# A two-layer decoder trunk in fp32: new order of work at the start, at the layer's jump, at the end of each feed-forward part and in the last norm

## Chip, cores, metric

The kernel runs on one core of one Trainium2 chip. The metric is the device time of one execution in microseconds (us), the median over several runs.

## What is computed

The reference is a decoder trunk of two layers over 1024 prompt positions and 8 sample positions, 1032 columns in all, with 1024 features. Cut to what matters here:

```python
for l in range(DEPTH):                      # DEPTH = 2
    h = _rmsnorm(x, w['norm_mix_g'][l])
    proj = jnp.einsum('bld,de->ble', h, w['w_in'][l])
    ...                                     # RG-LRU | retention | SSD heads on slices of proj
    x = x + jnp.einsum('blm,md->bld', mix, w['w_out'][l])
    h = _rmsnorm(x, w['norm_ffn_g'][l])
    gu = jnp.einsum('bld,df->blf', h, w['ffn_w_up'][l])
    gate, up = gu[..., :D_FF], gu[..., D_FF:]           # D_FF = 2816
    gate, ffn_buf = _causal_dwconv(gate, st_ffn_conv[l], w['ffn_conv_w'][l], w['ffn_conv_b'][l])
    x = x + jnp.einsum('blf,fd->bld', jax.nn.gelu(gate) * up, w['ffn_w_down'][l])
y = _rmsnorm(x, w['norm_final_g'])
```

The states of the convolutions and of the three recurrences are outputs too.

## The kernel before

Activations lie transposed: 128 features on the partitions, 1032 columns along a row, `x` as eight such tiles. Every large product is made in three passes of the tensor engine on numbers split into a high and a low part (`three`: w_hi by h_hi, w_hi by h_lo, w_lo by h_hi), over column groups of 344, so 9 matmul instructions of 128x344 for each pair of a weight tile and an activation tile (`three_wide`). The weights come in slots of 128x1024 (8 weight tiles): SP loads slot s into `w_raw[s % 2]`, GpSimd splits it into `w_hi` and `w_lo` (L649, L652), TensorE uses it and gives it free (`w_used0`, `w_used1`). There are 110 slots in a layer: 32 of the input projection, 12 of the output projection and 66 of the feed-forward part. So GpSimd can split a slot only when TensorE has left the one two before it.

The norm is not applied to `h`: ScalarE makes `h_hi` = x by gain (L1052) and the squares (L1048), VectorE makes `h_lo` (L1318) and adds the squares up in `rstd` (L1312, L1315). TensorE sums them over the partitions (`token_sums`, L750), VectorE and ScalarE take the root (`token_norm`), TensorE spreads the result over the partitions (`spread_rstd`, L759), and VectorE multiplies products by it when it takes them out of PSUM (`evict`, L1349).

A layer runs like this. (1) The first two input slots, tiles 24 and 25, are made together: for each feature tile k first slot 1, then slot 0 (from L913 on). Both are taken out of PSUM by VectorE with the factor `rstd` (L1631, L1633). Ahead of them stand the token sums, the `dt` products (L931) and the spread. (2) The other input slots and the output slots are dealt by a planner (`schedule`, `PLAN`) to six units of recurrent work, L0, L1 (RG-LRU), S0, S1 (SSD), R0, R1 (retention); projected tiles go to DRAM (`proj`) and are loaded again into `raw` or `pt` for convolutions and gates. SP issues all these loads in one queue, in program order, with a wait ahead of each: `load_conv` waits for `conv_done` where it uses a buffer again, and weight loads (`weights`, L373) stand behind it. (3) The feed-forward part: 11 blocks of 256 features. The loop makes, in each of its 10 turns, the four up slots of block b+1 and then the two down slots of block b (4 output tiles each). The two down slots of the last block come behind the loop. VectorE and ScalarE turn an up result into `y_hi`, `y_lo` (`up_part`, `y_part`, `ffn_block`) and VectorE adds each down result to `x` (L1834, L1843). Behind the last block `refresh` makes the next norm's squares and `h_hi`, `h_lo` tile by tile between those additions. After two layers the last norm follows, and eight tiles of output leave by `ev`, a buffer of two (L1853).

At the layer's jump the first two slots of the next layer are split by GpSimd like all others; the second one's buffer is given free at the very end of the layer (L1029 to L1030):

```python
            pe.wait_ge(sg.sem("m_ready"), layer * RUSES + RUSES)
            pe.nop().then_inc(sg.sem("w_used1"), 1)
```

and TensorE begins the layer with a wait for slot 1 and for all of PSUM (L911, L912).

## Time and profile before

| | us |
|---|---|
| median of 3 runs | 2965.53 (2960.07 to 2966.77) |
| profiled execution, its own time | 2957.84 |
| its span, first to last instruction | 2955.9 |
| TensorE busy in the span | 2836.5 (96%) |
| VectorE busy | 1645.2 (56%) |
| GpSimd busy | 1019.8 (35%) |
| ScalarE busy | 582.0 (20%) |
| mean granted TensorE clock | 0.979 of full |

The sum of the prediction is made against the profiled execution. Its time stands 7.7 us below the median of the runs. Busy times are shares of the whole span; the difference of span and busy time on TensorE, 119 us, lies in a few stretches and many short gaps.

### The profile page before, as it was taken

What the parts mean: (1) busy time and instruction counts of PE and PEld (TensorE: products, weight loads), DVE (VectorE), ACT (ScalarE), POOL (GpSimd) and SP (SyncE); (2) the same over time, 40 slices, a digit from 0 to 9 for tenths busy, and PEclk for the clock granted to TensorE, in tenths of its full rate; (3) what the DMA queues carried; (4) which work ended last, traced back from release to release, by engine and by line L of the source; (5) the groups of instructions that cost most, each with busy time, mean ns of one, the idle gap of its engine ahead of it and who ended that gap; (6) DMA issues with size and microseconds to landing.
All of it is one profiled execution on the core that took longest, in us unless ns stands there. A gap on an engine that the chain in (4) does not pass through costs nothing.

```text
span 2955.9 us, 46968 instructions
## 1 busy us (share of the span) xinstructions
PE 2836.5 (96%) x18164; PEld 2772.3 (94%) x18164; DVE 1645.2 (56%) x2122; ACT 582.0 (20%) x887; POOL 1019.8 (35%) x444
## 2 busy tenths in 40 slices
PE   7999999989999999999799999999999999999995
PEld 6999999979999999999789999988899999999995
DVE  4658886366444544444645587855664444444446
ACT  3333231113100111111213342211221111100002
POOL 2433233213343434444324333231233444434340
PEclk9999999989999999999999999999999999999997
DMA  4324334311111111111123234244011111111112
GB/s 154 114 78 144 108 123 160 121 61 38 51 44 49 44 49 50 43 50 43 54 79 105 93 137 138 96 151 138 30 46 49 50 43 50 43 50 43 50 43 77
DMA packets 75816, 227.94 MB, mean 77 GB/s; under 512 B 18672, under 2 KB 19696, under 8 KB 74624
## 3 DMA queue, kind: packets, MB, share of 16 engines
q1 hardware_dynamic: 73760, 219.77, 22.4%
q10 hardware_dynamic: 1920, 6.34, 0.7%
q8 instruction: 86, 1.41, 0.2%
q14 instruction: 50, 0.41, 0.0%
HBM read 180.63 MB, written 45.96 MB: 77 GB/s over the span
## 4 chain that ended last, share of the span: by engine, by line
PE 86%; DVE 7%; issue 4%; DMA 1%; ACT 1%; PEld 1%; POOL 0%; SPq 0%; DVEq 0%; ACTq 0%; POOLq 0%; PEldq 0%
PE ps L670 26%; PE ps L672 25%; PE ps L671 25%; PE ps L780 1%; DVE sb_pt L1362 1%; PE ps L838 1%; PE ps L803 1%; PE ps L901 1%; DVE sb_x L1352 1%; PE ps L884 0%; PE ps L815 0%; PE ps L814 0%; PE ps L902 0%; PE ps L759 0%; DMA sb_ch<-cos 0%
## 5 line engine op out<-in xcount | busy, mean ns | idle before, releaser
L670 PE MATMUL ps<-sb_h_hi,sb_w_hi 128*128 128x344 f32 x3744 | 1215.1, 325 | 32.0 <-DVE sb_h_lo L1318 15.1
L671 PE MATMUL ps<-sb_h_lo,sb_w_hi 128*128 128x344 f32 x3744 | 1201.6, 321 | 0.0
L672 PE MATMUL ps<-sb_h_hi,sb_w_lo 128*128 128x344 f32 x3744 | 1201.3, 321 | 0.0
L649 POOL TENSOR_TENSOR sb_w_hi<-sb_w_raw,sb_ones 128x1024 fp32r<-128x1024 f32 x220 | 426.9, 1941 | 1861.3 <-PEq L1011 877.9
L670 PEld LDWEIGHTS ps<-sb_h_hi,sb_w_hi 128*128 128x128 f32 x3744 | 709.6, 190 | 41.6 <-issue 16.7
L671 PEld LDWEIGHTS ps<-sb_h_lo,sb_w_hi 128*128 128x128 f32 x3744 | 709.4, 189 | 1.1
L672 PEld LDWEIGHTS ps<-sb_h_hi,sb_w_lo 128*128 128x128 f32 x3744 | 709.4, 189 | 0.0
L652 POOL TENSOR_TENSOR sb_w_lo<-sb_w_raw,sb_w_hi 128x1024 fp32r<-128x1024 f32 x220 | 592.8, 2695 | 17.3
L670 PE MATMUL ps<-sb_y_hi,sb_w_hi 128*128 128x344 f32 x1536 | 508.9, 331 | 37.3 <-DVE sb_y_lo L1824 12.3
L672 PE MATMUL ps<-sb_y_hi,sb_w_lo 128*128 128x344 f32 x1536 | 497.3, 324 | 0.0
L671 PE MATMUL ps<-sb_y_lo,sb_w_hi 128*128 128x344 f32 x1536 | 494.2, 322 | 0.0
L1834 DVE TENSOR_TENSOR sb_x<-ps,sb_x 128x1032 f32<-128x1032 f32 x160 | 197.2, 1233 | 256.1 <-PE ps L672 256.1
L670 PEld LDWEIGHTS ps<-sb_y_hi,sb_w_hi 128*128 128x128 f32 x1536 | 292.4, 190 | 46.0 <-issue 21.6
L671 PEld LDWEIGHTS ps<-sb_y_lo,sb_w_hi 128*128 128x128 f32 x1536 | 293.0, 191 | 1.1
L672 PEld LDWEIGHTS ps<-sb_y_hi,sb_w_lo 128*128 128x128 f32 x1536 | 292.8, 191 | 0.0
L1349 DVE TENSOR_TENSOR sb_ev<-ps,sb_rstd 128x344 f32<-128x344 f32 x180 | 89.6, 511 | 237.9 <-PE ps L672 219.5
L1283 ACT ACTIVATE sb_y_hi<-sb_pt 128x1032 fp32r<-128x1032 f32 x44 | 47.1, 1071 | 804.0 <-DVE sb_pt L1820 803.9
L1794 DVE TENSOR_TENSOR sb_raw<-ps,sb_rstd 128x1032 f32<-128x1032 f32 x44 | 54.3, 1234 | 254.6 <-PE ps L672 254.3
L1812 DVE TENSOR_TENSOR sb_pt<-ps,sb_rstd 128x1032 f32<-128x1032 f32 x44 | 54.2, 1233 | 232.8 <-PE ps L672 232.8
L1352 DVE TENSOR_TENSOR sb_x<-ps,sb_x 128x344 f32<-128x344 f32 x264 | 126.8, 509 | 54.9 <-PE ps L672 54.3
L1801 DVE SCALAR_TENSOR_TENSOR sb_pt<-sb_raw,sb_par,sb_pt 128x1024 f32<-128x1024 f32 x88 | 129.4, 1470 | 7.2 <-DVE sb_pt L1804 6.2
L1276 ACT ACTIVATE sb_pt<-sb_raw,sb_par 128x1032 f32<-128x1032 f32 x44 | 55.3, 1256 | 328.0 <-DVE sb_raw L1794 328.0
(243 smaller groups left out, 2222.0 us busy)
## 6 DMA issues: line engine op xcount, KB each, us to landing
sb_w_raw<-w SPq DMA_DIRECT2D x222, 512.0 KB, 3.5
proj<-sb_ev SPq DMA_DIRECT2D x64, 516.0 KB, 3.5
sb_raw<-proj SPq DMA_DIRECT2D x32, 516.0 KB, 4.5
sb_pt<-proj SPq DMA_DIRECT2D x28, 516.0 KB, 6.6
sb_ch<-cumT SPq DMA_DIRECT2D x32, 256.0 KB, 4.0
sb_x<-x SPq DMA_DIRECT2D x8, 516.0 KB, 8.7
y<-sb_ev SPq DMA_DIRECT2D x8, 516.0 KB, 2.7
sb_raw<-ssd_state SPq DMA_DIRECT2D x4, 1024.0 KB, 6.3
```

Of the source, the lines that this page charges most:

```text
L649: nc.gpsimd.tensor_tensor(w_hi[:, q, :], w_raw[:, q, :], ones[:, 0:1].to_broadcast([P, 1024]), ALU.mult).then_inc(sg.sem("w_hi_done"), 1)
L652: nc.gpsimd.tensor_tensor(w_lo[:, q, :], w_raw[:, q, :], w_hi[:, q, :].bitcast(F32), ALU.subtract).then_inc(*sg.on("w_split_done", q))
L670: mm(o, wh, ah, start=first, stop=False)
L671: mm(o, wh, al, start=False, stop=False)
L672: return mm(o, wl, ah, start=False, stop=last)
L1276: af(pt[:, j, :], raw[:, j, 2:T + 2], ACT.Identity, bias=wt[3], scale=wt[2]).then_inc(*sg.on("ffn_tap", (tag, j)))
L1349: v.tensor_tensor(ev[:, EV[i], gc(g)], o, rstd[:, gc(g)], ALU.mult).then_inc(*sg.on(f"p_free{r % NB}", r))
L1352: v.tensor_tensor(x[:, mo, gc(g)], o, x[:, mo, gc(g)], ALU.add).then_inc(*sg.on(f"p_free{r % NB}", r))
L1794: v.tensor_tensor(g3(raw[:, j, 2:T + 2]), ffn_bank(r)[:, :, 0:TG], g3(rstd[:]), ALU.mult).then_inc(*sg.on("m_free", ("ffn", r)))
L1801: stt(pt[:, j, 0:SEQ], raw[:, j, k:k + SEQ], w, pt[:, j, 0:SEQ], ALU.mult, ALU.add).then_inc(*line.step())
L1812: v.tensor_tensor(g3(pt[:, 2 + j, :]), ffn_bank(r)[:, :, 0:TG], g3(rstd[:]), ALU.mult).then_inc(*sg.on("m_free", ("ffn", r)))
L1834: v.tensor_tensor(g3(x[:, mo, :]), ffn_bank(r)[:, :, 0:TG], g3(x[:, mo, :]), ALU.add).then_inc(*sg.on("m_free", ("ffn", r)))
```

## The change

It does the following.

- Start: SP loads weight slot 0 first, ScalarE's own queue loads `x` tile 0, slot 1 comes behind `x` tile 3. ScalarE and VectorE split slots 0 and 1 of the first layer; GpSimd starts with the third slot. `h_hi` and `h_lo` of all tiles come before the squares and their sums. TensorE runs 20 products of `ones` by `ones` (128x128) ahead of its first work.
- First two slots of each layer: slot 0 with tiles 0 to 3, slot 1 with tiles 0 to 3, slot 0 with tiles 4 to 7, slot 1 with tiles 4 to 7. TensorE starts them without the last PSUM bank group and with slot 0 alone. The last sum of squares is added at the layer's top (`sums_done`). ScalarE takes tiles 24 and 25 out of PSUM without `rstd`, and VectorE multiplies them in SBUF later (`t0_scaled`, `t1_scaled`). The spread comes behind the first piece of tile 26.
- Loads: the second use of `raw` in units L0, L1 (gates) and S0, S1 (convolution tiles 2 and 3) is issued by ScalarE instead of SP. In S0, S1 `silu` of tile 1 comes ahead of the tap of tile 2.
- End of the feed-forward part: the loop has 9 turns. Then: the last block's four up slots; the first down slot of block 9; the first down slot of block 10, on `y` parts that are kept in `h_hi`, `h_lo` tiles 6 and 7; and two slots "both", each with two output tiles summed over the four feature tiles of both blocks in PSUM. The number of matmul instructions is the same; `x` gets 12 additions there instead of 16.
- Last norm: the token sum is made in two parts, seven tiles' squares and the last tile's; the spread goes to PSUM banks 0 to 2 in two steps, VectorE reads it there, and the eight output tiles have eight places (`ev` and six of `pt`), the first and the last in two parts.

The core of the difference:

```diff
+        sp.dma_start(w_raw[:, 0, :], io["w"][0]).then_inc(sg.sem("w_raw0"), 16)
         sp.dma_start(gains[:], io["gains"]).then_inc(*sg.on("gains_loaded", None, 16))
-        sp.dma_start(w_raw[:, 0, :], io["w"][0]).then_inc(sg.sem("w_raw0"), 16)
-        sp.dma_start(x[:, 0, :], io["x"][0]).then_inc(*sg.on("x_loaded0", None, 16))
-        sp.dma_start(w_raw[:, 1, :], io["w"][1]).then_inc(sg.sem("w_raw1"), 16)
         for m in range(1, KD):
             sp.dma_start(x[:, m, :], io["x"][m]).then_inc(*sg.on(f"x_loaded{m}", None, 16))
+            if m == 3:
+                sp.dma_start(w_raw[:, 1, :], io["w"][1]).then_inc(sg.sem("w_raw1"), 16)
...
-                if u < 4:
-                    for j in (2, 3):
-                        load_conv(u, j, t0 + j)
...
+        pairs = DEPTH * SLOTS // 2 - 1
+        with pool.Fori(0, pairs) as i, sg.loop("split", pairs, i):
+            for q in range(2):
+                pool.wait_ge(sg.sem(f"w_raw{q}"), i * 16 + 32)
+                pool.wait_ge(sg.sem(f"w_used{q}"), i + (1 + q))
...
+        pe.wait_ge(*sg.after("ones_ready"))
+        for _ in range(20):
+            mm(ps[:, 3, 0:128], ones[:], ones[:], start=True, stop=True)
         with pe.Fori(0, DEPTH) as layer, sg.loop("layer", DEPTH, layer):
+            def tile_k(bank0, q, k, last):
+                w = slice(k * P, (k + 1) * P)
+                return three_wide(ps[:, bank0:bank0 + 3, :], w_hi[:, q, w], w_lo[:, q, w], h_hi[:, k, :], h_lo[:, k, :],
+                                  k == 0, last)
...
+            slot_ready(0)
+            pe.wait_ge(sg.sem("m_free"), layer * RUSES + (M0 - 1))
+            for k in range(4):
+                pe.wait_ge(sg.sem("h_split"), layer * (2 * KD) + (k + 1))
+                ins = tile_k(4, 0, k, False)
+                if k == 0:
+                    ins.then_inc(sg.sem("w_used1"), 1)
             slot_ready(1)
             pe.wait_ge(sg.sem("m_free"), layer * RUSES + M0)
-            for k in range(KD):
+            for k in range(4):
+                tile_k(0, 1, k, False)
+            for k in range(4, KD):
                 pe.wait_ge(sg.sem("h_split"), layer * (2 * KD) + (k + 1))
-                w = slice(k * P, (k + 1) * P)
-                ins = three_wide(ps[:, 0:3, :], w_hi[:, 1, w], w_lo[:, 1, w], h_hi[:, k, :], h_lo[:, k, :],
-                                 k == 0, k == KD - 1)
-                if k == KD - 1:
-                    ins.then_inc(*sg.on("t1_ready"))
-                ins = three_wide(ps[:, 4:7, :], w_hi[:, 0, w], w_lo[:, 0, w], h_hi[:, k, :], h_lo[:, k, :],
-                                 k == 0, k == KD - 1)
+                ins = tile_k(4, 0, k, k == KD - 1)
             ins.then_inc(*sg.on("t0_ready"))
+            for k in range(4, KD):
+                ins = tile_k(0, 1, k, k == KD - 1)
+                if k == 4:
+                    ins.then_inc(sg.sem("w_used0"), 1)
+            ins.then_inc(*sg.on("t1_ready"))
...
+            pe.wait_ge(*sg.after("sums_done"))
+            token_sums("mix", "w_used1")
             pe.wait_ge(*sg.after("wdt_ready"))
             for k in range(KD):
                 for g, (c0, n) in enumerate(DT):
                     ins = mm(ps[32 * g:32 * g + 8, 3, 0:n], A("wdt", 8 * k, 8), x[:, k, c0:c0 + n],
                              start=k == 0, stop=k == KD - 1)
             ins.then_inc(*sg.on("dt_done"))
-            pe.wait_ge(*sg.after("dt_taken"))
-            spread_rstd("mix")
             pe.wait_ge(*sg.after("t1_free"))
             run([("in", 26, 0)])
...
+            run([("in", 26, 1)])
+            pe.wait_ge(*sg.after("rstd_ready", "mix"))
...
+                n, pieces = {"up": (KD, 1), "down": (2, 4), "down_last": (2, 4), "both": (4, 2)}[kind]
...
+            for j in range(4):
+                ffn_slot("up", j % 2, END + 4 + j, 0, SLOTS - 8 + j)
+            pe.wait_ge(sg.sem("ffn_split"), layer * FB + (FB - 1))
+            ffn_slot("down", 0, END + 8, 0, SLOTS - 4)
             pe.wait_ge(sg.sem("ffn_split"), layer * FB + FB)
+            ffn_slot("down_last", 1, END + 12, 0, SLOTS - 3)
             for j in range(2):
-                ffn_slot("down", j, 4 + 4 * j, 12 * (FB - 1), 48 + j, 6 * (FB - 1))
-            pe.wait_ge(sg.sem("m_ready"), layer * RUSES + RUSES)
-            pe.nop().then_inc(sg.sem("w_used1"), 1)
-        pe.wait_ge(sg.sem("h_split"), (2 * DEPTH + 1) * KD)
+                ffn_slot("both", j, END + 16 + 2 * j, 0, SLOTS - 2 + j)
...
+        pe.wait_ge(*sg.after("sq_used", ("next", KD - 2)))
+        token_sums("most")
+        pe.wait_ge(*sg.after("sq_tile", ("next", KD - 1)))
+        for c in range(NCH + 1):
+            s = slice(c * CHUNK, min((c + 1) * CHUNK, T))
+            ins = mm(ps[0:s.stop - s.start, 3, c:c + 1], ev[:, 1, s], ones[:, 0:1], start=True, stop=True)
+        ins.then_inc(*sg.on("tok_sum", "last"))
         pe.wait_ge(sg.sem("m_free"), DEPTH * RUSES + M0)
-        token_sums("last")
-        spread_rstd("last")
+        for _ in range(4):
+            mm(ps[:, 4, 0:128], ones[:], ones[:], start=True, stop=True)
+        pe.wait_ge(*sg.after("tok_rstd", "last"))
+        for c in range(NCH + 1):
+            n = min(CHUNK, T - c * CHUNK)
+            o = ps[:, c // 4, (c % 4) * CHUNK:(c % 4) * CHUNK + n]
+            ins = mm(o, rt[0:n, c:c + 1].to_broadcast([n, P]), ident[0:n, 0:n], start=True, stop=True)
+            if c in (3, NCH):
+                ins.then_inc(*sg.on("spread", c // 4 - c // NCH))
...
+        def load_s(u, j):
+            tile = TILE0[UNITS[u]] + j
+            act.wait_ge(*sg.after(f"ev_stored{EV[tile]}", tile))
+            act.wait_ge(*sg.after("conv_done", (u, j - 2)))
+            act.dma_start(raw[:, j - 2, 3:T + 3],
+                          io["proj"][tile]).then_inc(*sg.on(f"raw_turn{j - 2}", (u, j), 16))
...
+        act.dma_start(x[:, 0, :], io["x"][0]).then_inc(*sg.on("x_loaded0", None, 16))
+        act.wait_ge(*sg.after("ones_ready"))
+        af(rgc[:, 0, 0:1], ones[:, 0:1], ACT.Square)
+        act.wait_ge(sg.sem("w_raw0"), 16)
+        af(w_hi[:, 0, :], w_raw[:, 0, :], ACT.Identity).then_inc(*sg.on("first_hi", 0))
         act.wait_ge(*sg.after("gains_loaded"))
         for m in range(KD):
+            if m == 4:
+                act.wait_ge(sg.sem("w_raw1"), 16)
+                af(w_hi[:, 1, :], w_raw[:, 1, :], ACT.Identity).then_inc(*sg.on("first_hi", 1))
             act.wait_ge(*sg.after(f"x_loaded{m}"))
-            refresh(m, 0, "start")
+            part(m, 0, "start")
+        for m in range(KD):
+            square(m, "start")
...
+            act.wait_ge(*sg.after("t0_ready"))
+            af(g3(ev[:, 0, :]), ps[:, 4:7, 0:TG], ACT.Identity).then_inc(*sg.on("t0_free"))
+            act.wait_ge(*sg.after("t1_ready"))
+            af(g3(ev[:, 1, :]), ps[:, 0:3, 0:TG], ACT.Identity).then_inc(*sg.on("t1_free"))
...
+                load_s(u, 2)
                 silu(u, 0)
+                load_s(u, 3)
+                silu(u, 1)
                 tap_s(u, 2)
-                silu(u, 1)
...
+        def first_lo(q):
+            dve.wait_ge(sg.sem(f"w_raw{q}"), 16)
+            dve.wait_ge(*sg.after("first_hi", q))
+            if q == 0:
+                dve.wait_ge(sg.sem("w_split_done"), FREE)
+            v.tensor_tensor(w_lo[:, q, :], w_raw[:, q, :], w_hi[:, q, :].bitcast(F32),
+                            ALU.subtract).then_inc(sg.sem("w_split_done"), 1)
+        first_lo(0)
         dve.wait_ge(*sg.after("gains_loaded"))
         for m in range(KD):
+            if m == 4:
+                first_lo(1)
             dve.wait_ge(*sg.after(f"x_loaded{m}"))
-            refresh(m, 0, "start")
+            part(m, 0, "start")
+        for m in range(KD - 1):
+            add_square(m, "start")
...
+            v.tensor_tensor(rstd[:], rstd[:], ev[:, 1, :], ALU.add).then_inc(*sg.on("sums_done"))
...
+            up_part(FB - 1, "end", END + 4, 0)
+            y_product("end", END + 7, 0)
+            for mo in range(2):
+                down(mo, END + 8 + mo, 0, "end")
+            y_rest("end")
+            for mo in range(2, 4):
+                down(mo, END + 8 + mo, 0, "end")
+            dve.wait_ge(*sg.after("ffn_split", "end"))
             v.nop().then_inc(*sg.on("par_free"))
             for mo in range(KD):
-                r = 4 + mo
-                dve.wait_ge(sg.sem("m_ready"), layer * RUSES + 12 * (FB - 1) + (r + 1))
-                v.tensor_tensor(g3(x[:, mo, :]), ffn_bank(r)[:, :, 0:TG], g3(x[:, mo, :]),
-                                ALU.add).then_inc(*sg.on("m_free", ("last", r)))
-                if mo >= 1:
+                if mo < 4:
+                    dve.wait_ge(sg.sem("m_free"), layer * RUSES + (END + 9 + mo + M0))
+                if mo == KD - 1:
+                    add_square(mo - 1, "next")
+                down(mo, END + 12 + mo, 0, "last")
+                if mo == KD - 1:
+                    part(mo - 1, layer * 2 + 2, "next")
+                elif mo >= 1:
                     refresh(mo - 1, layer * 2 + 2, "next")
-            refresh(KD - 1, layer * 2 + 2, "next")
-        token_norm("last")
-        take_rstd("last")
+            part(KD - 1, layer * 2 + 2, "next")
...
+        wide = ps[:, 0:3, :].rearrange("p a n -> p (a n)")
         for m in range(KD):
-            if m >= 2:
-                dve.wait_ge(*sg.after(f"y_stored{m % 2}", m - 2))
-            stt(ev[:, m % 2, :], x[:, m, :], gains[:, 2 * DEPTH * KD + m:2 * DEPTH * KD + m + 1], rstd[:],
-                     ALU.mult, ALU.mult).then_inc(*sg.on("y_ready", m))
+            gp = gains[:, 2 * DEPTH * KD + m:2 * DEPTH * KD + m + 1]
+            for n, s in enumerate(parts(m)):
+                if m == 0:
+                    dve.wait_ge(*sg.after("spread", n))
+                stt(out_tile(m)[:, s], x[:, m, s], gp, wide[:, s], ALU.mult, ALU.mult).then_inc(*sg.on("y_ready", (m, n)))
...
+        rows = [256 * b + P * k for b in (FB - 2, FB - 1) for k in range(2)]
         seq = ups(0)
-        for b in range(FB - 1):
+        for b in range(FB - 2):
             seq += ups(b + 1) + downs(b)
-        seq += downs(FB - 1)
+        seq += ups(FB - 1) + [downs(FB - 2)[0], downs(FB - 1)[0]]
+        seq += [fin_slot(down, rows, (4, 5)), fin_slot(down, rows, (6, 7))]
```

Below, names of the kernel before and after are as the programs print them; `[waits ...]` names semaphores, and a line number is one of the kernel it comes from. 
SP at the start of unit S0 (`sb_raw<-proj` are the convolution's tiles, `sb_pt<-proj` the gates, `sb_w_raw<-w` weight slots), before:

```order
L423 DMA sb_raw<-proj 128x1032 [waits conv_done]
L423 DMA sb_raw<-proj 128x1032 [waits ev_stored1,conv_done]
L482 ISA
L400 REGISTER_ALU [waits y_split]
L430 DMA sb_pt<-proj 128x1032 [waits ev_stored0]
L430 DMA sb_pt<-proj 128x1032 [waits ev_stored1]
L559 ISA
L497 DMA sb_ch<-cumT 128x512 [waits cumT_stored]
L497 DMA sb_ch<-cumT 128x512 x2
L395 REGISTER_ALU
L397 DMA proj<-sb_ev 128x1032 [waits p_free2]
L371 REGISTER_ALU
```

and after (`L442` loads the gates now, `L388` the weights):

```order
L479 ISA
L415 REGISTER_ALU [waits y_split]
L442 DMA sb_pt<-proj 128x1032 [waits ev_stored0]
L442 DMA sb_pt<-proj 128x1032 [waits ev_stored1]
L553 ISA
L494 DMA sb_ch<-cumT 128x512 [waits cumT_stored]
L494 DMA sb_ch<-cumT 128x512 x2
L410 REGISTER_ALU
L412 DMA proj<-sb_ev 128x1032 [waits p_free2]
L386 REGISTER_ALU
L388 ISA [waits w_split_done]
L388 DMA sb_w_raw<-w 128x1024
```

The two loads with `conv_done` ahead of them are gone from SP, and the next weight load (the DMA that follows the rows shown before, the last row after) waits for no convolution any more.

VectorE from the last turn of the feed-forward loop into what follows it, before (`L1834` and `L1843` add a down result to `x`):

```order
L1833 REGISTER_ALU
L1834 TENSOR_TENSOR sb_x<-ps,sb_x 128x1032 [waits m_ready]
L1820 TENSOR_TENSOR sb_pt<-sb_pt 128x1032 [waits ffn_gelu,m_free]
L1820 TENSOR_TENSOR sb_pt<-sb_pt 128x1032 [waits ffn_gelu]
L1824 TENSOR_TENSOR sb_y_lo<-sb_pt,sb_y_hi 128x1032 [waits ffn_hi] x2
L1829 REGISTER_ALU
L1829 COMPARE_AND_BRANCH
L1838 ISA
L1842 REGISTER_ALU [waits ffn_split]
L1843 TENSOR_TENSOR sb_x<-ps,sb_x 128x1032 [waits m_ready]
L1842 REGISTER_ALU
L1843 TENSOR_TENSOR sb_x<-ps,sb_x 128x1032 [waits m_ready]
```

and after, from the last block's products on (`L1932` gelu by up, `L1946` an addition to `x`, `L1940` the low part):

```order
L1932 TENSOR_TENSOR sb_pt<-sb_pt 128x1032 [waits ffn_gelu,m_free]
L1932 TENSOR_TENSOR sb_pt<-sb_pt 128x1032 [waits ffn_gelu]
L1945 REGISTER_ALU
L1946 TENSOR_TENSOR sb_x<-ps,sb_x 128x1032 [waits m_ready] x2
L1940 TENSOR_TENSOR sb_h_lo<-sb_pt,sb_h_hi 128x1032 [waits ffn_hi] x2
L1945 REGISTER_ALU
L1946 TENSOR_TENSOR sb_x<-ps,sb_x 128x1032 [waits m_ready]
L1945 REGISTER_ALU
L1946 TENSOR_TENSOR sb_x<-ps,sb_x 128x1032 [waits m_ready]
L1966 ISA
L1945 REGISTER_ALU [waits ffn_split,m_free]
L1946 TENSOR_TENSOR sb_x<-ps,sb_x 128x1032 [waits m_ready]
```

Before, the last low part (`L1824`) stands behind the eighth addition and directly ahead of the first one that needs it; after, four additions of the block before lie around it (`L1946`), and it writes to `sb_h_lo`.

## Rows read from the trace of the kernel before

**Rows 1.** The page, busy times of TensorE; and the windows view, one stretch of the feed-forward loop.

```profile
PE 2836.5 (96%) x18164; PEld 2772.3 (94%) x18164; DVE 1645.2 (56%) x2122; ACT 582.0 (20%) x887; POOL 1019.8 (35%) x444
...
800.00:1110.00 310.00, 310.00 (x1977) 310.00 (x1976) 144.31 (x110) 30.57 (x27) 127.01 (x56) 1.00 0.14 46
```

**Rows 2.** Waits of TensorE: for whom, us in total, times, longest.

```profile
PE ps L670 <- DVE sb_h_lo L1318: 15.1, 1, 15.1
...
PE ps L670 <- POOL sb_w_lo L652: 13.1, 3, 6.8
PE ps L670 <- DVE sb_y_lo L1824: 12.3, 2, 6.2
PE ps L750 <- DVE sb_h_lo L1318: 8.6, 1, 8.6
...
PE ps L670 <- DVE sb_ev L1631: 4.5, 2, 2.2
...
PE ps L670 <- DVE sb_x L1843: 3.4, 3, 2.6
```

**Rows 3.** Timeline, start: begin, us, instruction, [idle before <- releaser]; GpSimd, ScalarE, VectorE.

```profile
5.04 1.89 POOL L649 TENSOR_TENSOR sb_w_hi<-sb_w_raw,sb_ones 128x1024 fp32r<-128x1024 f32 x1 [4.59 <-DMA sb_w_raw<-w]
...
6.85 1.28 ACT L1048 ACT_TABLE_LOAD   x1 [6.85 <-DMA sb_x<-x]
...
9.11 1.14 ACT L1052 ACTIVATE sb_h_hi<-sb_x,sb_gains 128x1032 fp32r<-128x1032 f32 x1
...
9.34 2.42 DVE L1312 COPY sb_rstd<-sb_ev 128x1032 f32<-128x1032 f32 x1 [8.25 <-ACT sb_ev L1048]
11.68 3.37 DVE L1318 SCALAR_TENSOR_TENSOR sb_h_lo<-sb_x,sb_gains,sb_h_hi 128x1032 fp32r<-128x1032 f32 x1
...
16.12 1.28 DVE L1318 SCALAR_TENSOR_TENSOR sb_h_lo<-sb_x,sb_gains,sb_h_hi 128x1032 fp32r<-128x1032 f32 x1
```

**Rows 4.** Timeline of TensorE: the first two slots and the token sums behind them.

```profile
15.11 0.65 PE L670 MATMUL ps<-sb_h_hi,sb_w_hi 128*128 128x344 f32 x1 [15.11 <-DVE sb_h_lo L1318]
...
19.57 0.47 PE L670 MATMUL ps<-sb_h_hi,sb_w_hi 128*128 128x344 f32 x1
...
40.01 1.94 PE L750 MATMUL ps<-sb_ones,sb_rstd 128*128 128x1 f32 x17
```

**Rows 5.** Timeline of TensorE: the spread and the first piece of tile 26.

```profile
48.73 2.36 PE L759 MATMUL ps<-sb_con,sb_rt 128*128 128x128 f32 x18 [1.57 <-ACT sb_ch L1183]
53.32 0.42 PE L670 MATMUL ps<-sb_h_hi,sb_w_hi 128*128 128x344 f32 x1 [2.23 <-DVE sb_ev L1631]
...
57.20 0.43 PE L670 MATMUL ps<-sb_h_hi,sb_w_hi 128*128 128x344 f32 x1
```

**Rows 6.** Timeline, unit S0 of layer 0: SP's queue, then GpSimd.

```profile
236.09 18.99 SPq L423 DMA_DIRECT2D sb_raw<-proj  x4
...
267.66 1.90 POOL L649 TENSOR_TENSOR sb_w_hi<-sb_w_raw,sb_ones 128x1024 fp32r<-128x1024 f32 x1 [16.86 <-DMA sb_w_raw<-w]
```

**Rows 7.** Timeline, end of layer 0 and the jump: TensorE, then GpSimd.

```profile
1440.28 0.65 PE L670 MATMUL ps<-sb_y_hi,sb_w_hi 128*128 128x344 f32 x1 [6.15 <-DVE sb_y_lo L1824]
...
1474.84 0.65 PE L670 MATMUL ps<-sb_h_hi,sb_w_hi 128*128 128x344 f32 x1 [6.76 <-POOL sb_w_lo L652]
...
1468.32 2.99 POOL L649 TENSOR_TENSOR sb_w_hi<-sb_w_raw,sb_ones 128x1024 fp32r<-128x1024 f32 x1 [9.11 <-PEq L1029]
1471.38 3.22 POOL L652 TENSOR_TENSOR sb_w_lo<-sb_w_raw,sb_w_hi 128x1024 fp32r<-128x1024 f32 x1
```

**Rows 8.** Timeline, the last norm: TensorE, then VectorE; and the page's line on the output's stores.

```profile
2927.80 3.70 PE L750 MATMUL ps<-sb_ones,sb_rstd 128*128 128x1 f32 x18 [8.60 <-DVE sb_h_lo L1318]
2932.30 4.30 PE L759 MATMUL ps<-sb_con,sb_rt 128*128 128x128 f32 x18 [0.80 <-DVE sb_rt L1328]
...
2938.04 2.50 DVE L1853 SCALAR_TENSOR_TENSOR sb_ev<-sb_x,sb_gains,sb_rstd 128x1032 f32<-128x1032 f32 x2
...
y<-sb_ev SPq DMA_DIRECT2D x8, 516.0 KB, 2.7
```

185 lines of the change are left out of this document (109 added, 76 removed).

## Prediction

> **What bounds the kernel now.** The page comes first: TensorE is busy 2836.5 us of 2955.9, VectorE 56%, GpSimd 35% [rows 1]. In the feed-forward stretch from 800 to 1110 us it is busy without a gap, at the full granted clock [rows 1]. So the change, which keeps the matmuls of the large products, can take at most what lies outside that busy time, 119 us, and what TensorE loses at half clock. The list of TensorE's waits says where to look [rows 2]: 15.1 us at the very start, three waits for GpSimd's split (13.1), two for the low part of y (12.3), one of 8.6 in the last norm, two for the eviction of tiles 24 and 25 (4.5), three for x (3.4). The timelines of these places give the chains. The sum is made against the profiled execution, 2957.8 us.
>
> **Start.** TensorE's first product begins at 15.11 [rows 4]. The chain to it: x tile 0 is there at 6.85, a table load of 1.28, a square, `h_hi` (1.14) from 9.11, then on VectorE a copy of 2.42 and the low part of 3.37, from 11.68 [rows 3]. Later low parts take 1.28 [rows 3]; only the first two VectorE instructions are stretched, and GpSimd's splits run beside them. After the change the table load lies ahead of the data, the copy and the square are behind, and GpSimd does nothing there. The new chain: the first weight slot's data were used from 5.04 on [rows 3] and x tile 0 is asked for at the same time from a second queue. I take both as landed between 5.0 and 6.85, at 5.9, since two transfers share the engines. Then the high split of the slot, about an `h_hi` (1.14), `h_hi` itself 1.14, and the low part 1.28: TensorE starts at about 9.4 (8.6 to 10.5). The low split (one more 1.2) lies beside `h_hi`. That saves 5.7.
>
> By the Trainium skill, "DMA: Bandwidth & Descriptors", section on issuing engines, DMAs issued from several engines run on the same 16 DMA engines and interleave. By that rule x tile 0 gains only issue time and the weight slot is slowed by it; it speaks for the upper end of my landing time, and would give 10.5 instead of 9.4. No row here shows two queues at once.
>
> Clock: from 15.11 to 19.57 there are 16 products 0.29 apart, then 0.158 (the other 128 or so take until 40.01) [rows 4], so the cold start costs 2.1. The 20 idle products are 40 records; 18 such records took 2.36 at full clock [rows 5] and 4.30 at half [rows 8], so they fill 1.2 us to between 6.4 and 10.8. I take it that the clock is up when the real work starts: another 2.1. If it never rises in them, they end at 10.8, TensorE starts 1.4 later, and the 2.1 stay. A group (one weight tile by one activation tile) takes 9 x 0.158 = 1.42, more than VectorE's 1.28 for the next low part, so TensorE is not starved; slot 1 is needed only 5.7 us in, when its split by VectorE, between low parts 4 and 5, is done. Sum for the start: 7.8 (3 to 9).
>
> **Ahead of tile 26, in both layers.** TensorE waits 1.57 for ScalarE's copies, then 2.23 for VectorE's eviction, and then makes 13 products at half clock until 57.20 (13 x 0.13 = 1.6) [rows 5]; the second layer has the same waits [rows 2]. After, the bank group is freed by ScalarE while TensorE still makes the sums, and the first piece of tile 26 stands where the waits were. Its split is in time: the slot's buffer is free after the 13th of the 16 tile groups, 4.3 us before their end, and the token sums and `dt` products follow (7.2 us from 40.01 to the 1.57 wait before 48.73 [rows 4, 5]), against a split of 4.3. I book 5.4 twice, 10.8. VectorE has `rstd` some 7 us later in relation to TensorE's place than before; the only one who would feel it is the first gate product of unit L0, and there VectorE's convolution was done some 8 us ahead. I leave that margin uncosted, and take up to 3 us of it into the range.
>
> **S units.** SP stands in `load_conv` from 236.09 to 255.08 and the weight loads stand behind it; so GpSimd is idle 16.86 us for its data and begins at 267.66 [rows 6]. Two such waits reach TensorE: 13.1 less the 6.76 of the jump [rows 2, 7] is 6.3, and one of them is followed by about 1.3 at half clock. After, the weight load follows the spill of tile 6 and comes some 10 us earlier, which covers it. What is late next: `tap` of tile 2 now waits for `silu` of tile 1, which puts the third convolution about 1.6 later and uses up most of a slack of 2.8 on the first transposes. I book 6.0 of 7.6; lowest 2.
>
> **End of the feed-forward part, in both layers.** TensorE waits 6.15 for the last low part [rows 7], the same in layer 1 (12.3 in two, [rows 2]), and each time makes 11 products at half clock, 1.4 to 1.6. In the new order 11.4 us of products (72 x 0.158) lie between the last up slot and the first use of the new y. In these VectorE has an eviction, two products, two additions and two low parts of about 1.2 each, 8.5 in all with ScalarE's parts beside them: 2.9 in hand. Then 3.4 of waits for x [rows 2] go too, since VectorE's work per tile (addition, square sum and low part, three instructions near the 1.28 of [rows 3], 3.5 in a row) now meets 5.7 us of products for each of the last four tiles; the first four may lag but have two bank groups and that time to catch up. 12.3 + 3.0 + 3.4 + 0.5 for the clock after them: 19.2.
>
> **The jump.** TensorE waits 6.76 for GpSimd, whose split of slot 1 takes 2.99 + 3.22 from the moment TensorE leaves the layer [rows 7], and then makes 21 products at half clock (2.8). After, slot 0's split is done long before, and TensorE has 5.7 us of work on it. Slot 1's buffer is given free 1.5 us into that. With a split of 4.3 (no VectorE work beside it) to 6.2 (as in [rows 7]) slot 1 is ready at 5.8 to 7.7, needed at 5.7: a wait of 0.1 to 2.0, I take 0.9. Sum: 8.6.
>
> The stretch of the split is what "SBUF: State Buffer" of the Trainium skill, section on the shared port pair, gives: GpSimd and a VectorE instruction with two SBUF inputs lock each other out. By that rule VectorE's two low parts and the last square sum, which now run just then, would each hold the split up, and the wait would be 2.0, the sum 7.5.
>
> **Last norm.** TensorE's last product ends at 2927.80 - 8.60 = 2919.20 [rows 8], 36.7 before the end of the span. After, from that point: addition 1.2, square 1.1, nine one-column products 1.9 to 3.7, root and reciprocal 1.1, first part of the spread 1.1 to 1.9 (half of 2.36 or 4.30, [rows 5, 8]), eight output tiles at 1.27 (2.50 for two, [rows 8]) 10.2, and the store of a half tile, under the 2.7 of a whole one [rows 8]. That is 18.7 to 21.8; I take 20.7, since eight stores of 516 KB in 10 us leave the DMA engines no room. Saved: 16.0. The copies of `rstd` and three waits for `ev` are what goes.
>
> **Sum.** 7.8 + 10.8 + 6.0 + 19.2 + 8.6 + 16.0 = 68.4. From 2957.8 that is 2889.4. The median of the runs shown lies 7.7 above the profiled execution, so the forecast for the median is 2965.5 - 68.4 = 2897. ScalarE's new work (two evictions, 16 DMA issues) is costed at nothing: it is busy 20% [rows 1].
>
> **Rivals.**
> 1. *The waits move.* TensorE is freed of one wait and meets VectorE's next one, in L0 by the late `rstd`, in the S units by the later convolutions, and at the jump. For it: VectorE is already what the S units wait for in many small places, and the gain there is then only the clock. Price: 6 us of the S term, 5 of the tile 26 term, 2 at the jump, 5 at the start for an idle clock and late data. That is 18 back, 2915. Chance 0.2.
> 2. *More comes than booked.* Full S term, start at 8.6, tail 18.7, and the median no further from the profile than 3 us: 2886. Chance 0.09.
> 3. *It is slower.* ScalarE now waits for `conv_done` and `ev_stored` in order, with `silu`, taps and the sigmoids' successors behind those waits, at 16 places. Each wait would have to cost TensorE over 68.4/16 = 4.3 us before the gain is gone; at 5.5 the time is 2985. Against it: ScalarE's own next instruction needs `conv_done` of the same tile anyway. Chance 0.02.
> 4. *It does nothing measurable*: the stalls are merely handed on, 2965. The start and the tail have nothing behind them to hand on to. Chance 0.02.
>
> The forecast itself has 0.67. Its own range, 2889 to 2907, is the sum of half the spreads of the start, S and last norm terms and 5 us for the median. The range with 8 in 10 takes in most of rival 1 and of 2: 2885 to 2915. A measurement of this kernel can tell about 0.2%, 6 us, from no change. Faster 0.96, same 0.02, slower 0.02.
>
> **What would show it.** First product of tile 24 at 8.6 to 10.5, at full clock, and the token sums at about 32; no wait ahead of tile 26; no wait for `w_lo` in the S units; none for a low part at the end of the feed-forward part; at the jump a single wait under 2 for `w_lo`; from TensorE's last large product to the end 21. It is wrong if TensorE's busy time grows by more than 3 us, if the S units show new waits for VectorE of over 2 each, or if the idle products still run when the first low part is ready.

## The result, and the profile after

The changed kernel takes 2928.7 us (median of 4 runs, 2927.0 to 2931.5), the kernel before 2965.7 beside it. The ratio is 0.988, 95% interval 0.9863 to 0.9897. So 37.0 us are saved, a little over half of the 68.4 that were forecast, and the time lies 14 above the upper end of the wide range (2885 to 2915). The profiled execution is the one of 2926.99, span 2925.2.

The page and TensorE's waits after the change, against [rows 1, 2]:

```profile
PE 2848.9 (97%) x18230; PEld 2785.7 (95%) x18230; DVE 1657.0 (57%) x2116; ACT 588.7 (20%) x894; POOL 1012.0 (35%) x440
```

```profile
PE ps L670 <- POOL sb_w_lo L652: 7.5, 3, 3.3
PE ps L670 <- DVE sb_y_lo L1659: 5.6, 2, 2.8
PE ps L802 <- DVE sb_pt L1491: 5.2, 2, 3.0
PE ps L770 <- ACT sb_pt L1146: 4.9, 2, 2.9
...
PE ps L670 <- DVE sb_x L1946: 4.1, 2, 2.1
```

The waits that the prediction named are gone from their places. Those for L1659 and L802 were there before (5.6 for the first in both profiles of the kernel before; 2.0 and 5.7 for the second). New are three for `w_lo` (two ahead of tile 27, 3.27 and 3.05, and one of 1.18 at the jump), two for ScalarE's `silu` in unit S0, one in each layer (2.02 and 2.90), and two for an addition at the end of the feed-forward part.

TensorE's busy time grew by 12.4, which the prediction had named as a sign that it is wrong. 9.4 of these are the idle products that the change adds (7.3 at the start, 2.1 in the last norm). And the busy time of the kernel before is no fixed number: its second profile has 2849.2 for the same 18164 instructions, 12.7 more, at a mean granted clock of 0.974 instead of 0.979. So this sign could tell nothing. The stretches of the program, measured on TensorE from mark to mark (first token sum, first gate product, and so on; the tail of a unit S begins with the first matmul of the group `ps<-sb_ch,sb_con`), show where the time went. The columns are layer 0 / layer 1; the second profile of the kernel before, and the changed kernel's second, come from the experiments below.

| stretch | before | before, second | after | after, second | booked | got, first pair |
|---|---|---|---|---|---|---|
| start to token sums of layer 0 | 40.0 | 40.4 | 32.1 | 32.2 | 7.8 | 7.9 |
| token sums to L0's gates | 50.8 / 50.8 | 50.8 / 50.8 | 49.9 / 49.7 | 51.2 / 49.7 | 10.8 | 1.9 |
| to the tail of S0 | 238.8 / 236.5 | 238.3 / 238.4 | 235.8 / 237.5 | 236.8 / 236.4 | 6.0 (all S) | 2.1 |
| to the tail of S1 | 122.1 / 122.0 | 122.0 / 122.6 | 123.0 / 121.7 | 123.7 / 123.0 | | -0.7 |
| to R0's first product | 50.5 / 52.0 | 53.9 / 54.9 | 54.5 / 53.7 | 54.8 / 53.4 | 0 | -5.8 |
| R units, to the token sums | 215.8 / 210.1 | 216.4 / 218.7 | 216.1 / 216.4 | 215.7 / 214.4 | 0 | -6.7 |
| feed-forward part of layer 0 and jump | 782.3 | 782.4 | 767.9 | 767.7 | 18.2 | 14.5 |
| feed-forward part of layer 1, to its last large product | 747.3 | 747.1 | 742.3 | 740.8 | 9.6 | 5.0 |
| from there to the end | 37.0 | 37.1 | 24.5 | 24.4 | 16.0 | 12.5 |

Start, ScalarE, then VectorE, then TensorE, against [rows 3, 4]:

```profile
5.82 1.06 ACT L1233 ACTIVATE sb_w_hi<-sb_w_raw 128x1024 fp32r<-128x1024 f32 x1 [3.13 <-DMA sb_w_raw<-w]
6.79 4.30 ACT L1090 ACTIVATE sb_h_hi<-sb_x,sb_gains 128x1032 fp32r<-128x1032 f32 x4
...
6.98 1.23 DVE L1676 TENSOR_TENSOR sb_w_lo<-sb_w_raw,sb_w_hi 128x1024 fp32r<-128x1024 f32 x1 [5.88 <-ACT sb_w_hi L1233]
...
1.15 7.34 PE L911 MATMUL ps<-sb_ones 128*128 128x128 f32 x40 [1.15 <-DVE sb_ones L1666]
9.46 0.42 PE L670 MATMUL ps<-sb_h_hi,sb_w_hi 128*128 128x344 f32 x1 [0.97 <-DVE sb_h_lo L1410]
...
32.14 1.94 PE L750 MATMUL ps<-sb_ones,sb_rstd 128*128 128x1 f32 x17
```

Slot 0 is there at 5.80 and `x` tile 0 at 5.98, the first product comes at 9.46, and the products are 0.16 apart from the second on, the spacing at full clock: the chain went as forecast, step by step.

Ahead of tile 27, SP's queue, GpSimd, TensorE:

```profile
47.54 0.33 SPq L412 DMA_DIRECT2D proj<-sb_ev  x1
48.23 0.33 SPq L388 DMA_DIRECT2D sb_w_raw<-w  x1
...
53.37 1.89 POOL L649 TENSOR_TENSOR sb_w_hi<-sb_w_raw,sb_ones 128x1024 fp32r<-128x1024 f32 x1 [20.16 <-DMA sb_w_raw<-w]
...
57.74 0.57 PE L670 MATMUL ps<-sb_h_hi,sb_w_hi 128*128 128x344 f32 x1 [3.27 <-POOL sb_w_lo L652]
```

GpSimd is idle for 20 us, for a load of weights that stands on SP behind the spill of tile 24. The spill now waits for the scaled tile (L1741 ends near 47.5). The diff shows it in two lines, which the prediction passed over: `main(FIRST[0])` now stands ahead of `main(FIRST[1])`. `main` asks for the slots below SLOT+3 before its spill and for slot SLOT+3 behind it. Tile 25, the first one before, has SLOT 1, and tile 24, the first one now, has SLOT 0. So slot 3's load was ahead of every spill before and is behind one now.

End of the feed-forward part of layer 0, VectorE, GpSimd, TensorE, against [rows 7]:

```profile
1406.30 5.21 DVE L1932 TENSOR_TENSOR sb_pt<-sb_pt 128x1032 f32<-128x1032 f32 x2
1411.44 2.36 DVE L1946 TENSOR_TENSOR sb_x<-ps,sb_x 128x1032 f32<-128x1032 f32 x2
...
1405.16 1.90 POOL L649 TENSOR_TENSOR sb_w_hi<-sb_w_raw,sb_ones 128x1024 fp32r<-128x1024 f32 x1 [6.92 <-PEq L1033]
1407.14 3.28 POOL L652 TENSOR_TENSOR sb_w_lo<-sb_w_raw,sb_w_hi 128x1024 fp32r<-128x1024 f32 x1
...
1412.71 0.47 PE L670 MATMUL ps<-sb_y_hi,sb_w_hi 128*128 128x344 f32 x1 [2.05 <-DVE sb_x L1946]
```

The two products take 5.21 together beside GpSimd's split, the additions that free the banks come late, and TensorE waits 2.05.

The jump, GpSimd and TensorE, against [rows 7]:

```profile
1456.88 1.89 POOL L649 TENSOR_TENSOR sb_w_hi<-sb_w_raw,sb_ones 128x1024 fp32r<-128x1024 f32 x1 [8.70 <-PE ps L672]
1458.86 3.24 POOL L652 TENSOR_TENSOR sb_w_lo<-sb_w_raw,sb_w_hi 128x1024 fp32r<-128x1024 f32 x1
...
1462.23 0.42 PE L670 MATMUL ps<-sb_h_hi,sb_w_hi 128*128 128x344 f32 x1 [1.18 <-POOL sb_w_lo L652]
```

The end, TensorE, then VectorE and SP's queue, against [rows 8]:

```profile
2900.86 1.96 PE L750 MATMUL ps<-sb_ones,sb_rstd 128*128 128x1 f32 x18
2903.52 2.77 PE L1060 MATMUL ps<-sb_ones,sb_ev 128*128 128x1 f32 x18 [0.70 <-ACT sb_ev L1086]
2906.22 2.08 PE L1064 MATMUL ps<-sb_ones 128*128 128x128 f32 x8
2908.09 3.84 PE L1069 MATMUL ps<-sb_con,sb_rt 128*128 128x128 f32 x18
...
2911.97 1.95 DVE L1997 SCALAR_TENSOR_TENSOR sb_ev<-sb_x,sb_gains,ps 128x520 f32<-128x520 f32 x2 [1.18 <-PE ps L1069]
2913.84 7.41 DVE L1997 SCALAR_TENSOR_TENSOR sb_pt<-sb_x,sb_gains,ps 128x1032 f32<-128x1032 f32 x7
...
2915.21 6.88 SPq L629 DMA_DIRECT2D y<-sb_pt  x7
```

### The profile page after: what moved, and what is told of

The parts are those of the page before. It is cut to its first block, busy times and chain, and to the rows that moved or that the text cites. A ratio compares the mean times of both kernels' runs of the same rounds, so it can differ in the third digit from the quotient of the medians.

```text
span 2925.2 us, 46986 instructions
## 1 busy us (share of the span) xinstructions
PE 2848.9 (97%) x18230; PEld 2785.7 (95%) x18230; DVE 1657.0 (57%) x2116; ACT 588.7 (20%) x894; POOL 1012.0 (35%) x440
## 4 chain that ended last, share of the span: by engine, by line
PE 59%; issue 24%; POOL 8%; DVE 5%; DMA 2%; ACT 1%; SPq 0%; POOLq 0%; DVEq 0%; ACTq 0%
PE ps L670 17%; PE ps L672 17%; PE ps L671 17%; POOL sb_w_hi L649 5%; POOL sb_w_lo L652 3%; DVE sb_pt L1454 1%; PE ps L782 1%; DMA sb_ch<-cos 1%; DMA sb_w_raw<-w 1%; PE ps L840 1%; PE ps L784 1%; PE ps L903 1%; PE ps L787 0%; PE ps L904 0%; PE ps L805 0%
## 5 line engine op out<-in xcount | busy, mean ns | idle before, releaser
L670 PE MATMUL ps<-sb_h_hi,sb_w_hi 128*128 128x344 f32 x3840 | 1246.8, 325 | 14.5 <-POOL sb_w_lo L652 7.5
L671 PE MATMUL ps<-sb_h_lo,sb_w_hi 128*128 128x344 f32 x3840 | 1233.1, 321 | 0.0
L672 PE MATMUL ps<-sb_h_hi,sb_w_lo 128*128 128x344 f32 x3840 | 1232.4, 321 | 0.0
L670 PEld LDWEIGHTS ps<-sb_h_hi,sb_w_hi 128*128 128x128 f32 x3840 | 728.2, 190 | 25.3 <-issue 8.9
L671 PEld LDWEIGHTS ps<-sb_h_lo,sb_w_hi 128*128 128x128 f32 x3840 | 728.1, 190 | 1.1
L672 PEld LDWEIGHTS ps<-sb_h_hi,sb_w_lo 128*128 128x128 f32 x3840 | 728.2, 190 | 0.0
L670 PE MATMUL ps<-sb_y_hi,sb_w_hi 128*128 128x344 f32 x1440 | 477.8, 332 | 20.3 <-DVE sb_x L1444 10.5
L672 PE MATMUL ps<-sb_y_hi,sb_w_lo 128*128 128x344 f32 x1440 | 466.8, 324 | 0.0
L671 PE MATMUL ps<-sb_y_lo,sb_w_hi 128*128 128x344 f32 x1440 | 463.9, 322 | 0.0
L1946 DVE TENSOR_TENSOR sb_x<-ps,sb_x 128x1032 f32<-128x1032 f32 x168 | 206.7, 1231 | 247.5 <-PE ps L672 247.5
L670 PEld LDWEIGHTS ps<-sb_y_hi,sb_w_hi 128*128 128x128 f32 x1440 | 274.2, 190 | 27.8 <-DVE sb_x L1444 12.5
```

The costliest lines, as they stand in the source:

```text
L670: mm(o, wh, ah, start=first, stop=False)
L671: mm(o, wh, al, start=False, stop=False)
L672: return mm(o, wl, ah, start=False, stop=last)
L1946: v.tensor_tensor(g3(x[:, mo, :]), ffn_bank(r)[:, :, 0:TG], g3(x[:, mo, :]), ALU.add).then_inc(*sg.on("m_free", (tag, r)))
```

## Experiments

All edits are made on the changed kernel; the last run is the kernel before, unaltered. A ratio is to the kernel before on the same chip. The runs come from several chips, on which the medians of the kernel before lie between 2962.3 and 2966.7; so two times from different chips can be some us further apart, or nearer, than their ratios say.

**The changed kernel again** (a1).

> The changed kernel again, unaltered, as the base for its neighbours on the same chip. Both theories expect 2929 (2926 to 2932). If its profiled execution has the new waits again (3.27 and 3.05 ahead of tile 26, 2.05 twice at the end of the feed-forward part, 2.02 and 2.90 in the first S unit), they belong to the kernel and not to one execution.

2927.7 (2926.0 to 2929.4), ratio 0.9882 (0.9866 to 0.9899). The waits are there again: 3.32 and 3.07 ahead of tile 27 (the expectation says tile 26; the slot waited for is that of tile 27), 2.05 twice, 2.56 and 2.62 in S0. They belong to the kernel.

**Slot 3's load ahead of the first spill** (e1).

```diff
+            more(SLOT[FIRST[1]] + 3)
             main(FIRST[0])
             main(FIRST[1])
```

> SyncE asks for the weights of slot 3 ahead of the spill of tile 24. Theory (the load stood behind the spill's wait for the scaled tile, from the order of SyncE alone): slot 3's weight load issues near 15 instead of 48.2, the waits of 3.27 and 3.05 for its low part ahead of tile 26 go in both layers, and with them the 1.6 at half clock behind each; TensorE is 4.9 earlier at the gates of L0 in the first layer. Time 2919.5 if all of it lasts to the end (2929 - 9.5). Rival (the gain is handed on to VectorE, which has rstd late): the wait for the low part goes but a wait of 1.5 to 3 for VectorE stands within 15 us behind it, and the time is 2924 to 2929.

2926.3 (2918.5 to 2929.2), ratio 0.9866 (0.9847 to 0.9886): the rival by its time, though the wait for VectorE is 5.5 where it had 1.5 to 3. Slot 3 is split from 32.9 on, the wait for it is gone, and TensorE waits longer, a little later, for VectorE:

```profile
PE ps L671 <- DVE sb_ev L1442: 9.9, 3, 5.5
```

The stretch to L0's gates takes 53.3 and 50.9 instead of 51.2 and 49.7. VectorE's eviction stands behind its `dt` chain and a convolution; the chain waits for ScalarE, whose exponential stands behind two taps, and they wait for tiles 24 and 25 from memory (VectorE, then ScalarE, of this kernel):

```profile
61.88 0.20 DVE L1711 TENSOR_SCALAR sb_tok<-sb_tok 128x72 f32<-128x72 f32 x1 [6.03 <-ACT sb_tok L1270]
...
57.58 2.54 ACT L1141 ACTIVATE sb_pt<-sb_raw,sb_par 128x1032 f32<-128x1032 f32 x2 [11.50 <-DMA sb_raw<-proj]
```

**Slot 3's load, and the exponential ahead of the taps** (e8).

```diff
-            tap_l(0, 0)
-            tap_l(0, 1)
             act.wait_ge(*sg.after("dt_in"))
             ...
             af(tok[:, 3, :], tok[:, 3, :], ACT.Exp, scale=-1.0).then_inc(*sg.on("dt_exp"))
+            tap_l(0, 0)
+            tap_l(0, 1)
```

> Slot 3's load ahead of the spill of tile 24, as in e1, and ScalarE computes the exponential of dt ahead of the two taps, which wait for tiles 24 and 25 from memory. Theory (in e1 the split was in time, and TensorE then waited 5.5 near 75 for an eviction that stands on VectorE behind the dt chain, which waited 6.0 for ScalarE's exponential, which stood behind the taps): VectorE's dt chain starts near 58 instead of 61.9, the wait near 75 falls from 5.5 to 1.6 and that of the second layer likewise; TensorE is 4 earlier at the gates of L0 than in e1 in each layer; time 2917 to 2921. Rival (the convolution itself, waiting for the tap, is what holds the eviction): the wait stays above 4 and the time is that of e1, 2924 to 2928.

2921.8 (2916.7 to 2923.4), ratio 0.9847 (0.9831 to 0.9864): 6 below the changed kernel by the times and 10 by the ratios, whose intervals just miss each other. The time lies between the two theories. In the second layer the stretch falls to 45.8, 4 less, and its wait to 0.66. In the first the wait falls from 5.47 to 3.15, not to 1.6, and the stretch is 50.1 (49.9 and 51.2 in the changed kernel): the chain began at 59.6, 2.3 earlier, but the first convolution, 3.9 in the run before, now meets GpSimd's splits of the next slot:

```profile
64.95 7.52 DVE L1455 SCALAR_TENSOR_TENSOR sb_pt<-sb_raw,sb_par,sb_pt 128x1024 f32<-128x1024 f32 x3
...
72.95 0.50 PE L671 MATMUL ps<-sb_h_hi,sb_w_hi 128*128 128x344 f32 x1 [3.15 <-DVE sb_ev L1442]
```

**The tap of tile 2 ahead of `silu` of tile 1** (e2).

```diff
                 load_s(u, 2)
                 silu(u, 0)
+                tap_s(u, 2)
                 load_s(u, 3)
                 silu(u, 1)
-                tap_s(u, 2)
                 tap_s(u, 3)
```

> ScalarE in the S units: tap of tile 2 ahead of silu of tile 1 again, as it was in the kernel before, with the load of tile 3 between them. Theory (the new waits of 2.02 and 2.90 ahead of the transposes come from the tap that stands behind a silu, which makes VectorE's third convolution late): both go, VectorE's idle 1.85 ahead of that convolution goes, TensorE is 2 to 3 earlier at the S unit's end in each layer; time 2923 to 2925. Rival (VectorE's chain through the convolutions is slow because GpSimd's splits run beside it): waits of 1.5 to 3 stay, merely elsewhere, time 2927 to 2930.

2916.1 (2908.5 to 2917.5), ratio 0.9834 (0.9814 to 0.9854): 11.6 less than the changed kernel on the same chip, more than either theory gave. The stretch to the tail of S0 falls to 234.5 and 235.1, by 1.3 to 2.4; the waits ahead of the transposes fall to 0.80 and 1.20; VectorE's idle time ahead of the third convolution (1.85) becomes 0.39. VectorE in the first profile of the changed kernel, then in this run (the third and the last convolution):

```profile
247.08 0.17 DVE L1452 TENSOR_TENSOR sb_pt<-sb_pt,sb_par 128x8 f32<-128x8 f32 x1 [1.85 <-ACT sb_pt L1134]
253.35 5.92 DVE L1454 SCALAR_TENSOR_TENSOR sb_pt<-sb_raw,sb_par,sb_pt 128x1024 f32<-128x1024 f32 x3
...
244.80 3.92 DVE L1454 SCALAR_TENSOR_TENSOR sb_pt<-sb_raw,sb_par,sb_pt 128x1024 f32<-128x1024 f32 x3
249.95 0.17 DVE L1452 TENSOR_TENSOR sb_pt<-sb_pt,sb_par 128x8 f32<-128x8 f32 x1 [0.39 <-ACT sb_pt L1134]
250.04 7.55 DVE L1454 SCALAR_TENSOR_TENSOR sb_pt<-sb_raw,sb_par,sb_pt 128x1024 f32<-128x1024 f32 x3
```

The rival has its part too: beside GpSimd's split the last convolution still takes 7.55 where another takes 3.92, and waits of 0.80 and 1.20 stay. The order explains some 4 of the 11.6. Where the rest lies can be seen: TensorE's busy time is 2839.5 instead of 2848.5, 9.0 of the 10.1 by which the two profiled executions differ, with the same number of instructions, and the mean granted clock is 0.985 instead of 0.980. In all four executions it is 0.982 to 0.985, against 0.978 to 0.981 in the eight of the changed kernel. So TensorE spends less time at 1.2 GHz, most of it in layer 0's R units (210.4 instead of 215.7), which no edit touches. Why, no run here shows.

**The first addition between the two products** (e3).

```diff
             up_part(FB - 1, "end", END + 4, 0)
-            y_product("end", END + 7, 0)
-            for mo in range(2):
-                down(mo, END + 8 + mo, 0, "end")
+            for j in range(2):
+                y_product("end", END + 7, 0, (j,))
+                down(j, END + 8 + j, 0, "end")
             y_rest("end")
```

> VectorE at the end of the feed-forward part: the first addition stands between the two products instead of behind both. Theory (both products are stretched from 1.2 to 2.6 by GpSimd's split, so the addition that frees the banks ends 2.05 late): the wait of 2.05 for the addition goes in both layers, and the 1.6 at half clock behind it; the low parts of y are ready some 0.5 before they are needed; time 2929 - 7.3 = 2921.5. Rival (the chain as a whole is too long beside GpSimd, in whatever order): the wait comes back as one of 1 to 3 for the low part of y, and the time is 2926 to 2929.

2916.8 (2912.8 to 2919.4), ratio 0.9844 (0.9826 to 0.9862). Both waits are gone and none has come in their place. The two feed-forward stretches take 764.0 and 738.5. Against the second profile of the changed kernel (767.7 and 740.8) that is 6.0 less, against the first (767.9 and 742.3) 7.7; six of the eight profiles with the old order have the longer time in layer 1. So the 7.3 of the theory came. The time fell by more, 11.0. As in the run before, TensorE's busy time is shorter (2838.0, 10.5 less) and the mean granted clock is 0.985 in the profiled execution, 0.980 to 0.985 in the four. The two products of this kernel take 1.85 and 2.30, against 5.21 together:

```profile
1407.20 1.85 DVE L1932 TENSOR_TENSOR sb_pt<-sb_pt 128x1032 f32<-128x1032 f32 x1
1408.98 1.22 DVE L1946 TENSOR_TENSOR sb_x<-ps,sb_x 128x1032 f32<-128x1032 f32 x1
1410.12 2.30 DVE L1932 TENSOR_TENSOR sb_pt<-sb_pt 128x1032 f32<-128x1032 f32 x1
```

**No idle products in the last norm** (e4; the four of L1064 are left out).

> Last norm without the four idle products (8 records) between the column sums and the spread. Theory (they end at half clock 1.0 after the reciprocal is there, and the spread runs at half clock all the same): the spread starts 0.8 to 1.0 earlier, takes 3.8 as before, and from the last large product to the end are 23.4 instead of 24.4. Rival (they hold the clock up, and without them the column sums or the spread are slower): the spread takes over 4.5 and the tail stays 24.4 or grows.

A single execution: from the last large product to the end 24.1 instead of 24.4 (the changed kernel's second profile). The spread starts 0.15 behind the reciprocal instead of 0.96, but takes 4.14 instead of 3.96. The column sums took 2.90 instead of 2.62, but they stand ahead of the place of the idle products and can't owe it to them (2.77 in the changed kernel's first profile). So the idle products cost 0.8, and a part of it comes back. The end of 24.1 is there again in the two later runs without them (e9 and e10); the nine profiled executions with them have 24.4 or 24.5.

**No idle products at the start** (e5; the 20 are left out).

> Start without the 20 idle products. Theory (they take TensorE's clock up ahead of the first product): the first product stays at 9.2 to 9.5, since it waits for VectorE, the first 16 or so products run at half clock, and the token sums of the first layer come 2.1 later, near 34.2. Rival (the clock is up early for another reason, or the loss is hidden by VectorE's low parts): the first products are 0.158 apart all the same, or the token sums stay within 0.5 of 32.1.

```profile
9.46 0.66 PE L670 MATMUL ps<-sb_h_hi,sb_w_hi 128*128 128x344 f32 x1 [9.46 <-DVE sb_h_lo L1408]
...
12.47 0.32 PE L671 MATMUL ps<-sb_h_lo,sb_w_hi 128*128 128x344 f32 x1
```

The first product stays at 9.46, but ten starts are 0.27 or more apart (0.29 for most of them) until 12.47, then 0.16, the spacing of full clock. The token sums come at 33.50, 1.3 later than in the changed kernel. So by this execution the idle products are worth 1.3, not the 2.1 that I took from [rows 4]. Nor are they a safe means: of the eleven profiled executions with them ten have the token sums at 31.8 to 32.4, and one, that of e10 below, has them at 33.84, later than here. There the idle products ended at 7.38 and the first product began at 9.59 at full clock, and then the granted clock fell to half for 3.3 us (the last columns of a window are granted clock, DMA share and GB/s):

```profile
9.50:11.10 1.60, 1.51 (x9) 1.51 (x10) 1.60 (x3) 1.60 (x2) 0.00 (x0) 1.00 1.03 421
11.10:14.40 3.30, 3.30 (x14) 3.30 (x13) 3.30 (x4) 2.85 (x4) 0.00 (x0) 0.51 1.03 417
```

The execution as a whole took 2918.9, less than the changed kernel: R0 and the R units had short times, a warning against reading one execution's total.

**k asked for behind the evictions of y, ahead of both R units** (e6).

> Ahead of the R units ScalarE asks for k and its swapped rows behind the three evictions of y instead of right behind the sine table, so that q and the cosine table have the DMA engines to themselves first. Theory (the cosine table landed 14.5 after its issue, 11.1 before the change, since the loads of both queues now start within 0.4 of each other, and the rotation of q starts late for it): the rotation of q starts near 478 instead of 481.6 to 484, k lands before its turn, the wait of 3.3 ahead of the first product of R0 falls under 1 and TensorE is 2 to 4 earlier in R0 of each layer; 2922 to 2926. Rival (the bytes in all set the time, so k is just as late as the cosine was): the rotation of k waits for its data, the wait at R0 stays 3 or grows, time 2928 to 2933.

2928.8 (2926.8 to 2933.2), ratio 0.988 (0.9864 to 0.9897): the rival's time, by another way. The cosine table lands 9.7 after its issue instead of 14.4, VectorE begins at 476.68, and R0's wait falls to 0.91. But R1's k is late, a wait of 5.58 stands at 593.7 (4.91 at 2040.5), and everything is given back.

**All four edits that helped,** those of e8, e2, e3 and e4 (e9).

> The edits of e8 (slot 3 early, exponential first), e2 (tap of tile 2 ahead of silu), e3 (addition between the products) and e4 (no idle products at the end) together. Theory (each removes a wait at another place and all of them last to the end): the medians add, 2927.7 - 6.0 - 11.6 - 11.0 - 0.3 = 2899 (2895 to 2903). Rival (they free the same lead, which the R units' chains on VectorE take back once): the best single one plus what lies behind the R units, 2905 to 2910.

2909.5 (2899.6 to 2911.1), ratio 0.9801 (0.9774 to 0.9828). The sum of the single gains is not reached, and the median lies in the rival's range (2905 to 2910), though two of the five executions are below it. The stretches in which the edits lie keep what they gave alone (S0 234.5 / 234.7, feed-forward 763.9 / 738.6). R0 and the R units, 54.0 / 53.1 and 215.9 / 216.4, are what they are in most executions: the short R units of e2 and e3 don't add. But the profiled execution is the slowest of the five (2911.1, clock 0.982; the fastest, 2899.6, had 0.984), so these stretches speak for a slow one, and the rival's mechanism, a lead taken back once by VectorE, isn't shown by them.

**The two edits e2 and e3 alone** (e11).

> The edits of e2 and e3 alone, without slot 3's load, the exponential and the idle products. The four edits together gave 2909.5 (2899.6 to 2911.1) where the sum of the single ones was 2899. Theory (what e8 gained ahead of tile 26 is given back in L0 to R0, since VectorE is what the units wait for; the two edits at the S unit and at the feed-forward end carry all of e9): within 4 of e9, 2904 to 2911. Rival (e8's gain lasts, and e9's shortfall is that of e2 and e3, whose medians of four runs were low draws): 5 or more above e9's mean of 2906.7, 2912 to 2917.

2910.2 (2901.8 to 2916.8), ratio 0.9814 (0.9793 to 0.9835). That is the theory's range. By the medians these two carry all of e9; by the means (2910.9 against 2906.7), and by the ratios, 4 are left for the rest, as much as e8 gained in the second layer. The spread of five runs does not separate them.

**e9, and R0's k alone asked for later** (e10).

```diff
             act.dma_start(T1, io["sin"]).then_inc(*sg.on("sin_loaded", u, 16))
+            if u == 5:
+                load_keys_rest(u)
```

(`load_keys_rest` holds the five DMAs for k; for R0 it is called behind the evictions of y.)

> e9 and, for the unit R0 alone, k and its swapped rows asked for behind the evictions of y. Theory (in e6 the wait at R0 fell from 3.3 to 0.9, and the gain was lost again in a wait of 5.6 at R1, whose k came late; without that edit for R1 the gain stays): 2 to 5 below e9 in time, wait at R0 under 1.2, no wait over 2.6 near 590. Rival (VectorE's work from R0 on sets the pace and TensorE meets it again at R1 whatever comes before): within 2 of e9, and the waits for x near 590 grow by what R0 gave.

2902.1 (2899.1 to 2909.7), ratio 0.9792 (0.9767 to 0.9818), the fastest median, in the middle of e9's runs; the medians differ by 7.4 and the means by 2.8, where the theory had 2 to 5. The stretch to R0 falls from 54.0 / 53.1 to 51.2 / 51.2, R0's first product waits 0.57, and no wait near 590 is over 2.02: the theory's signs. In layer 0 the R units took 218.7, in layer 1 212.0, and the start lost 1.7 to the clock, as said above. Whether it beats e9 is open; both beat the changed kernel by 18 and more.

**The kernel before, once more** (b1).

> The kernel before, profiled once more. Theory (its profiled execution, 2957.8, was a low draw of the same kernel, and the difference to the median of 2965 lies in which waits of TensorE are followed by a stretch at half clock): a time of 2961 to 2967, with the same waits within 0.5 each at the start, tile 26, the jump and the end, and more products at half clock or longer waits in the R units. Rival (a fixed offset of the profiled execution): a time of 2957 to 2959 again.

2975.5, 17.6 more than the first profile and more than either theory had. The start, the stretch of tile 26, the feed-forward parts and the end agree within 0.4 (see the table). The difference lies in the R units of layer 1 (8.6), ahead of R0 (3.4 and 3.0) and in S0 of layer 1 (1.9). 12.7 of it are TensorE's busy time, for the same number of instructions and at a lower granted clock (0.974 against 0.979). VectorE, waiting for the cosine table ahead of R0, in the second profile; in the first it stood 2.61 and began at 485.01. Of these 6.0, 4.1 lie ahead of the table's issue (478.04 against 473.90) and 1.9 in its landing (12.9 behind it against 11.0):

```profile
491.02 1.24 DVE L1396 SCALAR_TENSOR_TENSOR sb_raw<-sb_raw,sb_ch 128x1032 f32<-128x1032 f32 x1 [7.99 <-DMA sb_ch<-cos]
```

## Why the prediction failed, by its own steps

Booked were 68.4; the first pair of profiles gives 30.9 (2957.8 - 2927.0). The steps that failed, with what each gave less than booked: the split of slot 3 ahead of tile 27 and the late `rstd` behind it (8.9), the S units (4.6), the two products at the end of the feed-forward part (8.3), the last norm (3.5). A further 12.4 is a difference in R0 and the R units that the kernel before shows against itself.

- **Start** (7.8, came 7.9): right in each step: data, high split, low part, 9.46 for 9.4, token sums at 32.14 for 32. The first product came 5.65 earlier and the time from it to the token sums fell by 2.2, for 5.7 and 2.1 booked. That the idle products alone give 2.1 isn't borne out: without them 1.3 was lost, and once they did not help. The weight slot took 5.1 from issue to landing with `x` tile 0 beside it, and 3.6 before; both had landed by 5.98, where 5.9 was taken. The Trainium skill's rule in "DMA: Bandwidth & Descriptors" (section on issuing engines: all transfers run on the same 16 engines and interleave) agrees with the slower slot; the 10.5 that the prediction made of it, from a landing at its upper end, did not come.
- **Ahead of tile 26** (10.8, came 1.9). The waits of [rows 5] went, as booked, and 3.27 and 3.05 for slot 3's low part came, each with 12 or 13 products at half clock behind it. The failed step is "its split is in time": I followed slot 2's buffer, and not slot 3's load on SP, past which the spill of tile 24 had been moved. Even with that mended nothing is gained in the first layer and 4 in the second (e1, e8): the next in line is VectorE's eviction behind the `dt` chain, and the margin that I left "uncosted" for the late `rstd` was used up here: the wait was 5.47, then 3.15.
- **S units** (6.0, came 1.4 in the first pair). The waits for `w_lo` are gone. The step that failed is the 1.6 of delay set against "a slack of 2.8": the tap behind `silu` let VectorE stand 1.85, as summed, but its last convolution met GpSimd's split and took 5.92 instead of 3.92 (and 1.58 instead of 0.17 for the short instruction ahead of it), so the slack was not there and TensorE waited 2.02 and 2.90. These waits over 2, put down to ScalarE's `silu` behind that convolution, are the prediction's own second sign of being wrong. e2 shows the part of the order; the part of the split is read from the rows alone, no run takes it away.
- **End of the feed-forward part and jump** (27.8 by two terms, came 19.5). The mechanism held, one duration did not, and it is the failed step: the products in "two products, two additions and two low parts of about 1.2 each". Their row in the kernel before, inside the loop, where a split runs beside them as it now does at the end, read 2.73 each:

```profile
L1820 DVE TENSOR_TENSOR sb_pt<-sb_pt 128x1032 f32<-128x1032 f32 x18 | 48.5, 2733 | 0.0
```

  I took the 1.2 from the old end, where GpSimd is idle (2.37 for the two). With 5.21 for the two the 2.9 in hand are gone before the first addition. "SBUF — State Buffer" in the Trainium skill (section on the two sides of SBUF: VectorE with two SBUF inputs and GpSimd lock each other out) was cited at the jump, where the low part took 3.24 and the wait was 1.18, against 0.9 booked and 2.0 by that rule. The traces agree with it here, by the 5.21 against 2.37, and I did not carry it to this place. The jump itself came: 14.5 in the stretch that ends with it less 5.0 in the one without leaves 9.5 (8.4 by the second profiles), for 8.6 booked. e3 takes back 6.0 to 7.7 of the 8.3.
- **Last norm** (16.0, came 12.5). Up to the reciprocal the chain took 6.1, within the 5.3 to 7.1 summed. The step that failed is the spread: its first half ended 2.9 behind the reciprocal, not 1.1 to 1.9, as idle products stood before it (0.96 from the reciprocal to its start, 0.15 without them) and it ran at half clock (granted 0.55 from 2906 to 2912). VectorE stood 1.18 for the second half, which the sum left out, and the span ends 3.9 behind VectorE's last output tile, where the sum had less than 2.7 for the store.
- **R0 and the R units** (not booked, -12.4). Against the second profile of the kernel before the same stretches give +0.6 and +2.6. The first profile was the lowest but one of 38 executions of that kernel (on several chips). So the change has no loss there that could be told from the kernel's own spread. I had seen that the profile lay 7.7 under the median, but added it to both kernels; only the kernel before had been so lucky (the changed kernel's profile is 1.7 under its median). The saving is taken from medians, and so 6.2 more than that of the first pair: 30.9 + 6.2 is, rounded, 37.0. That is arithmetic, not a cause; it says that against a typical execution some 31 are missing and not 37.5.

Rival 1, "the waits move", had the right mechanism at the tile 26 and the S places, and 18 for its price; at the jump and at the start it was not needed, and it lacked the feed-forward end and the tail. So its 2915 is 14 short as well. (Rival 2's 2886 is about 2888 by its own terms.) What stays open is why TensorE's clock fell less in e2 and e3, which gave 11.6 and 11.0 where their own stretches explain 4 and 6 to 8.

## What to carry to other kernels

Take the duration of an instruction from a row where the same neighbours run beside it, not from the place where it stood before the change. When a step moves on a queue, list every load that it now stands ahead of, slot by slot. And take two profiles of the kernel before: a stretch that differs between them by more than the effect cannot carry a term, nor refute one.

## What the runs showed that was not expected

One kernel's executions differ by up to 22 us (the kernel before: 2953.5 to 2975.5), while its feed-forward stretches repeat within 0.2. Most of the difference of two executions is time at half clock: 12.7 of 17.8 between the two profiles of the kernel before. It comes after waits of 2 to 3 us, and not every time. The wait of 2.05 at the end of layer 1 of the changed kernel was followed by 13 products at 1.2 GHz in the first profile (granted clock 0.64 in the next 2 us) and by one in the second (1.00), and the stretch took 742.3 and 740.8. The cosine table ahead of R0 landed 11.0 to 14.1 after its issue in the kernel before, 12.8 to 14.4 in the changed one, and 9.7 and 10.7 in e6, where k was asked for later.
